# The borders between layers 0, 1 and 2: the last eight k-tiles by token halves, the norm per token block, and the first 768 columns turned in parts

## What is computed

```python
for layer in range(DEPTH):                    # 0: dilated attention, 1: latent attention
    y = mixer(x, ...)                         # h = x @ w_in ... y @ w_out
    x = layer_norm(DEEPNORM_ALPHA * x + y, ln_g[layer], ln_b[layer])
for layer in range(DEPTH):                    # layers 2 and 3 of the kernel
    x = x + layer(x, ev_norm or od_norm, ...) # RMS norm ahead of w_in
```

## Time and profile before

| | |
|---|---|
| median of 3 runs | 2440.97 us (2440.07 to 2441.13) |
| the profiled execution | 2441.87 us, span 2440.1 us, mean granted TensorE clock 0.999 |
| TensorE matmul busy | 2419.8 us, 99% of the span, 12720 |
| TensorE weight load busy | 2064.6 us, 85% |
| VectorE busy | 1474.5 us, 60%; of it 953.0 in L1853 |
| ScalarE busy | 1184.4 us, 49%; of it 802.0 in L1261 |
| GpSimd busy | 144.6 us, 6%; of it 97.0 in L2687 |
| DMA | 416.68 MB, mean 171 GB/s |

### The profile page before, as it was taken

One profiled execution on the slowest core, in us unless ns is written; L12 is line 12 of the kernel. 1 busy time (PEld: TensorE's weight loads), 2 busy tenths in 40 slices (PEclk: granted clock), 3 DMA queues, 4 the chain that ended last, 5 costly groups with the idle time before them and its releaser, 6 DMA issues.

```text
span 2440.1 us, 31500 instructions
## 1 busy us (share of the span) xinstructions
PE 2419.8 (99%) x12720; PEld 2064.6 (85%) x12720; DVE 1474.5 (60%) x1936; ACT 1184.4 (49%) x1620; POOL 144.6 (6%) x124
## 2 busy tenths in 40 slices
PE   8999999999999999999999999999999999999999
PEld 7888888888888888888899878888888888888887
DVE  5747575757575757575556575555455566657654
ACT  5454444444444445344555455554444468645443
POOL 1101010101010101000000000000000010000000
PEclk9999999999999999999999999999999999999999
DMA  8555555555554555646554656555555564433344
GB/s 261 173 173 195 197 187 164 190 165 187 166 189 159 187 172 173 207 147 199 172 138 134 203 153 194 173 184 184 176 173 161 169 209 155 138 111 125 111 138 138
DMA packets 368469, 416.68 MB, mean 171 GB/s; under 512 B 28042, under 2 KB 298596, under 8 KB 367812
## 3 DMA queue, kind: packets, MB, share of 16 engines
q1 hardware_dynamic: 366692, 407.72, 52.4%
q0 software_dynamic: 1344, 6.89, 0.8%
q10 hardware_dynamic: 288, 0.05, 0.0%
HBM read 412.52 MB, written 2.10 MB: 170 GB/s over the span
## 4 chain that ended last, share of the span: by engine, by line
PE 96%; ACT 2%; DVE 1%; issue 1%; DMA 0%; POOL 0%; ACTq 0%; DVEq 0%
PE ps L617 19%; PE ps L619 19%; PE ps L618 19%; PE ps L648 15%; PE ps L647 7%; PE ps L1129 2%; PE ps L689 2%; PE ps L851 1%; PE ps L840 1%; PE ps L902 1%; PE ps L904 1%; PE ps L903 1%; PE ps L845 1%; PE ps L719 1%; PE ps L939 0%
## 5 line engine op out<-in xcount | busy, mean ns | idle before, releaser
L1853 DVE TENSOR_TENSOR wlo<-raw,whi 128x1024 fp32r<-128x1024 f32 (+1 forms) x768 | 953.0, 1250 | 637.6 <-ACT whi L1261 634.4
L1261 ACT CAST whi<-raw 128x1024 fp32r<-128x1024 f32 (+1 forms) x774 | 802.0, 1041 | 730.6 <-PE ps L619 545.2
L617 PE MATMUL ps<-whi,xx 128*128 128x512 f32 x2088 | 833.9, 399 | 0.0
L619 PE MATMUL ps<-whi,xx 128*128 128x512 f32 x2088 | 815.5, 391 | 0.0
L618 PE MATMUL ps<-wlo,xx 128*128 128x512 f32 x2088 | 814.3, 390 | 0.0
L648 PE MATMUL ps<-xx,whi 128*128 128x512 f32 x1536 | 538.9, 396 | 0.0
L619 PEld LDWEIGHTS ps<-whi,xx 128*128 128x128 f32 x2088 | 392.4, 188 | 83.6
L617 PEld LDWEIGHTS ps<-whi,xx 128*128 128x128 f32 x2088 | 393.1, 188 | 78.1 <-issue 1.6
L618 PEld LDWEIGHTS ps<-wlo,xx 128*128 128x128 f32 x2088 | 393.2, 188 | 76.4
L647 PE MATMUL ps<-xx,wlo 128*128 128x256 f32 x1440 | 405.7, 282 | 0.0
L648 PEld LDWEIGHTS ps<-xx,whi 128*128 128x128 f32 x1536 | 286.2, 188 | 63.2
(11 more groups left out here) (407 smaller groups left out, 1862.2 us busy)
## 6 DMA issues: line engine op xcount, KB each, us to landing
raw<-in_dsa_w_in SPq DMA_DIRECT2D x320, 512.0 KB, 4.5
raw<-in_ev_w_in SPq DMA_DIRECT2D x144, 512.0 KB, 4.6
raw<-in_od_w_in SPq DMA_DIRECT2D x96, 512.0 KB, 4.5
raw<-in_mla_w_in SPq DMA_DIRECT2D x48, 512.0 KB, 4.3
raw<-in_dsa_w_out SPq DMA_DIRECT2D x32, 512.0 KB, 4.6
raw<-in_mla_w_out SPq DMA_DIRECT2D x32, 512.0 KB, 4.8
raw<-in_ev_w_out SPq DMA_DIRECT2D x32, 512.0 KB, 4.6
raw<-in_od_w_out SPq DMA_DIRECT2D x32, 512.0 KB, 4.9
```

The source lines that it names most:

```text
L617: pe.matmul(o, xh[:, k, tokens[tb]], hi, start=start and s + l == 0, stop=False)
L619: m = pe.matmul(o, xl[:, k, tokens[tb]], hi, start=False, stop=stop and s + l == 2)
L1261: act.copy(whi[:, h % 4, :, 0:n] if n > FEW else few_high(h, n), whole_half(raw[:, u % 4, 2 * (h % 2):2 * (h % 2) + 2], n)).then_inc(hi_do ...
L1853: dve.tensor_tensor(wlo[:, h % 4, :, 0:n] if n > FEW else few_low(h, n), whole_half(raw[:, h // 2 % 4, 2 * (h % 2):2 * (h % 2) + 2], n), h ...
```

## The change

It touches the two borders 0 to 1 and 1 to 2.

- `last_unit` becomes `last_units` there: the last eight k-tiles of the last slab (four weight halves) run first for token block 0, then for block 1. Inside the second pass stand the transposes of parts (0, 0) and (1, 0) of the next layer's input. A part (g, tb) is pair g for token block tb; there are parts for g = 0, 1, 2 (`PARTS` = 3, 768 columns).
- Add, statistics, variance, power and shift are done for each block on its own (`measured`, `shift`).
- All columns are normed on ScalarE. The 768 first columns are turned without factor and bias; these are then applied behind the transposes, where they are numbers per partition: by ScalarE into `xh`, by VectorE into a scratch copy in `y` (`exact`), from which `xh` is subtracted. The numbers come from `vec`, for which four more rows are loaded early in layer 0; for layer 2 VectorE multiplies them once by the RMS gain.
- The same factor and bias on `x` itself, for the residual, move to GpSimd for the 768 columns: two instructions on 2 x 768 columns behind the transposes of part (2, 1). `add(0)` and `add(1)` of the layer, and `squares(2)`, wait for them.
- TensorE's slab takes pairs 0 to 2 for block 0, then for block 1, then 3 to 7 as before. `keep_warm` is not called there.

The diff, cut to its core:

```diff
+        def exact(g, tb):
+            o = (PARTS * tb + g) * S
+            return y[:, 0, o:o + S].rearrange("p (l t) -> p l t", l=2)
+
+        def part_of_bank(g, tb, l):
+            o = tb * S + l * P
+            return ps[:, 4 + g, o:o + P]
...
+            def turn_part(layer, g, tb):
+                pe.wait_ge(*ln_a.at(layer - 1, f"n{g}{tb}"))
+                for l in range(2):
+                    k = 2 * g + l
+                    m = pe.transpose(part_of_bank(g, tb, l), x[:, tb, k * P:(k + 1) * P], ident[:, :])
+                m.then_inc(*xt_p.up("t"))
+
             def first_slab(layer):
-                keep_warm(14, 7)
-                turn_x(layer, (0,))
-                keep_warm(6, 7)
-                for g in range(8):
+                def three(h, g, l, tb):
+                    k = 2 * g + l
+                    o, hi, lo = ps[:, tb, :], whi[:, h % 4, l], wlo[:, h % 4, l]
+                    pe.matmul(o, xh[:, k, tokens[tb]], hi, start=k == 0, stop=False)
+                    pe.matmul(o, xh[:, k, tokens[tb]], lo, start=False, stop=False)
+                    return pe.matmul(o, xl[:, k, tokens[tb]], hi, start=False, stop=k == KT - 1)
+
+                for g in range(PARTS):
+                    h = half[0] + g
+                    pe.wait_ge(*xt_d.at(xt_turn(layer, g, 0), "lo"))
+                    pe.wait_ge(lo_done, h + 1)
+                    three(h, g, 0, 0)
+                    if g == 2:
+                        turn_part(layer, 0, 1)
+                    three(h, g, 1, 0)
+                    if g == 0:
+                        turn_part(layer, 2, 0)
+                turn_part(layer, 1, 1)
+                for g in range(PARTS):
+                    pe.wait_ge(*xt_d.at(xt_turn(layer, g, 1), "lo"))
+                    three(half[0], g, 0, 1)
+                    three(half[0], g, 1, 1).then_inc(half_done, 1)
+                    half[0] += 1
+                    if g == 0:
+                        turn_part(layer, 2, 1)
+                    else:
+                        turn_x(layer, (g + 2,))
+                for g in range(PARTS, 8):
                     h = half[0]
-                    pe.wait_ge(*xt_d.at(8 * layer + g, "lo"))
+                    pe.wait_ge(*xt_d.at(xt_turn(layer, g), "lo"))
                     pe.wait_ge(lo_done, h + 1)
                     for l in range(2):
-                        k = 2 * g + l
-                        hi, lo = whi[:, h % 4, l], wlo[:, h % 4, l]
                         for tb in range(TB):
-                            o = ps[:, tb, :]
-                            pe.matmul(o, xh[:, k, tokens[tb]], hi, start=k == 0, stop=False)
-                            pe.matmul(o, xh[:, k, tokens[tb]], lo, start=False, stop=False)
-                            m = pe.matmul(o, xl[:, k, tokens[tb]], hi, start=False, stop=k == KT - 1)
-                        if k == 0:
-                            turn_x(layer, (1,))
+                            m = three(h, g, l, tb)
                     m.then_inc(half_done, 1)
                     half[0] += 1
                     if g < 6:
...
+            def last_units(k0, bank, layer):
+
+                for tb in range(TB):
+                    for s in range(4):
+                        h = half[0] + s
+                        pe.wait_ge(lo_done, h + 1)
+                        for l in range(2):
+                            k = k0 + 2 * s + l
+                            hi, lo = whi[:, h % 4, l], wlo[:, h % 4, l]
+                            o = ps[:, bank + tb, :]
+                            pe.matmul(o, xh[:, k, tokens[tb]], hi, start=False, stop=False)
+                            pe.matmul(o, xh[:, k, tokens[tb]], lo, start=False, stop=False)
+                            m = pe.matmul(o, xl[:, k, tokens[tb]], hi, start=False, stop=k == KT - 1)
+                            if tb and l == 0 and s >= 2:
+                                turn_part(layer + 1, s - 2, 0)
+                        if tb:
+                            m.then_inc(half_done, 1)
+                    if tb == 0:
+                        m.then_inc(*out_p.up("half"))
+                half[0] += 4
+
...
                     if layer == 2 or s == 0:
                         project(nothing, N, out_bank(s), fine=fine, then=turning_x(3) if s else None)
                         continue
-                    for j in range(3):
+                    for j in range(3 if layer == 3 else 2):
                         unit(nothing, 4 * j, N, out_bank(s), j == 0, False, fine)
-                    last_unit(12, out_bank(s))
+                    if layer == 3:
+                        last_unit(12, out_bank(s))
+                    else:
+                        last_units(8, out_bank(s), layer)
...
                 for u in range(8):
                     unit(side, fine, {0: more, 4: late}.get(u))
                 for s in range(2):
-                    project(nothing, fine, turning_x(3) if layer == 2 and s else None)
+                    if layer >= 2 or s == 0:
+                        project(nothing, fine, turning_x(3) if layer == 2 and s else None)
+                        continue
+                    for j in range(2):
+                        unit(nothing, fine)
+                    split(half[0] + AHEAD)
+                    half[0] += 4
             def first_slab(layer):
-                def normalise(q, tb):
-                    v = x[:, tb, q * N:(q + 1) * N]
+                def normalised(tb, c):
+                    v = x[:, tb, c]
                     return act.activation(v, v, ACT.Identity, bias=hrstd[:, tb:tb + 1], scale=rstd[:, tb:tb + 1])
-
-                act.wait_ge(*st_d.at(layer - 1, "h"))
-                normalise(1, 0)
-                turn_x(layer, (0,))
-                normalise(1, 1).then_inc(*ln_a.up("q0"))
-                normalise(2, 0)
-                normalise(2, 1).then_inc(*ln_a.up("q1"))
-                normalise(3, 0)
-                turn_x(layer, (1,))
-                normalise(3, 1).then_inc(*ln_a.up("q2"))
+                def part(g, tb):
+                    normalised(tb, slice(g * S, (g + 1) * S)).then_inc(*ln_a.up(f"n{g}{tb}"))
+
+                def quarter(q):
+                    for tb in range(TB):
+                        m = normalised(tb, slice(max(q * N, PARTS * S), (q + 1) * N))
+                    m.then_inc(*ln_a.up(f"q{q - 1}"))
+
+                def turned(g, tb):
+                    act.wait_ge(*xt_p.at(xt_turn(layer, g, tb), "t"))
+                    for l in range(2):
+                        k = 2 * g + l
+                        m = act.activation(xh[:, k, tokens[tb]], part_of_bank(g, tb, l), ACT.Identity,
+                                           bias=part_bias(layer, k), scale=part_gain(layer, k))
+                    m.then_inc(*xt_a.up("hi"))
+
+                split(half[0])
+                act.wait_ge(*st_d.at(layer - 1, "h0"))
+                act.wait_ge(*setup_d.at(0, "bias"))
+                part(0, 0)
+                split(half[0] + 1)
+                part(1, 0)
+                turned(0, 0)
+                turned(1, 0)
+                part(2, 0)
+                split(half[0] + 2)
+                turned(2, 0)
+                act.wait_ge(*st_d.at(layer - 1, "h1"))
+                part(0, 1)
+                part(1, 1)
+                turned(0, 1)
+                part(2, 1)
+                turned(1, 1)
+                quarter(1)
                 for g in range(8):
                     split(half[0] + AHEAD)
                     half[0] += 1
-                    if g < 6:
+                    if g == 0:
+                        turned(2, 1)
+                    elif g < 6:
                         turn_x(layer, (g + 2,))
+                    if g < 2:
+                        quarter(g + 2)
...
+                    elif layer < 3 and q < 2:
+                        dve.wait_ge(*ln_g.at(layer - 1, "bias"))
...
+                def measured(tb):
+                    c = slice(3 * N, D)
+                    if tb == 0:
+                        dve.wait_ge(*out_p.at(turn, "half"))
+                    else:
+                        dve.wait_ge(half_done, half[0])
+                    if turn == 0:
+                        dve.wait_ge(rows_in[3], 16)
+                    dve.scalar_tensor_tensor(out=x[:, tb, c], in0=x[:, tb, c], scalar=ALPHA, in1=ps[:, out_bank(3) + tb, :],
+                                             op0=ALU.mult, op1=ALU.add).then_inc(*add_d.up(f"add{3 + tb}"))
+                    dve.wait_ge(*add_d.at(turn, f"add{3 + tb}"))
+                    dve.bn_stats(stats[:, tb, 3], x[:, tb, c]).then_inc(*st_d.up(f"stats{tb}"))
+                    dve.wait_ge(*st_d.at(turn, f"stats{tb}"))
+                    dve.bn_aggr(mv[:, tb, :], flat(stats[:, tb])).then_inc(*st_d.up(f"aggr{tb}"))
+                    dve.wait_ge(*st_d.at(turn, f"aggr{tb}"))
```

(64 more changed lines are left out.)

82 lines of the change are left out of this document (40 added, 42 removed).

## The result

The changed kernel takes 2454.79 us (median of 5 runs, 2453.75 to 2455.46), the kernel before 2440.21 beside it: a ratio of 1.0058 [1.0047, 1.0068], 14.6 us slower. The profiled execution has a span of 2452.4 us and a mean granted clock of 0.996.

The account below looks back on a forecast made before the run. TensorE was taken to bound the kernel (96% of the last chain), with hardly any VectorE slack behind its filler. Terms 5.75 + 5.0 + 2 x 1.2 = 13.15 us, against the median 2440.97, gave 2454; range 2446 to 2460.

Parts of the forecast that it names:

- GpSimd's two instructions: Behind transposes (2,1), factor and bias of 1536 elements per partition each run 3.4 us, bounds 3.1 and 3.9.
- TensorE's idle: TensorE stands idle before the six matmuls of (2,1), some 7.2 us at each boundary.
- Pair g=3: Start of slab pair g=3, 5.75 us later than before at the first boundary, 5.0 at the second.
- the walk: Instruction-by-instruction costing of the new order from the last product to slab pair g=3, at each boundary.
- hold: GpSimd's two instructions block VectorE's SBUF work for their whole length, 3.4 us each, at each boundary.
- The walk without GpSimd: New order alone, up to pair g=3: gains 0.5 us at the first boundary, 1.2 at the second.
- Clock: Half clock behind TensorE's idle costs 1.2 us per boundary, between nothing and 2.0 with 0.1 behind it.
- The sum: Both boundaries' delays plus clock: 5.75 + 5.0 + 2 x 1.2 = 13.15 us, giving 2454.
- What costs nothing: Four more small loads and two tiny VectorE products early in layer 0 cost nothing, covered by over 20 us.
- (a): Rival: no mutual exclusion of GpSimd and VectorE bites at the boundaries; -1.7 us, 2439.3, chance 0.08.
- (b): Rival: filler time simply gone, TensorE goes from product to slab without a wait; -12 us, 2429, chance 0.03.
- (c): Rival: GpSimd gives the ports up between pieces of about 512 elements, or half overlaps PSUM work; +4.2, 2445, chance 0.08.

Follow-up runs that it names:

- e9: Changed kernel with GpSimd's two instructions released by the low part of pair 7, in layer 2 behind the relative-bias load's issue; 2447.44 us, ratio 1.0029.
- e8: Kernel before, plus two GpSimd multiplications of 1536 elements on scratch data, released by the bias of pair 3 in each slab; 2452.36 us, ratio 1.005.
- e3: Changed kernel with 26 identity matmuls of 128x128 ahead of TensorE's wait for the low part (2,1); 2452.22 us, ratio 1.0049.
- e1: Changed kernel with GpSimd's factor and bias applied to one column per token block instead of 768; 2441.49 us, ratio 1.0006.
- e5: Kernel of e2 with layer 2's relative-bias load issued behind x7 again instead of behind x2; 2441.42 us, ratio 1.0005.
- e6: Kernel of e5 with shift(1) right behind turned(1,0) and transposes (0,1) and (1,1) moved from pair 2 to pair 1; 2436.76 us, ratio 0.9986.
- e4: Changed kernel with each of GpSimd's two instructions cut into three of 512 elements; 2453.75 us.
- e2: Changed kernel with factor and bias of the first 768 columns moved from GpSimd to VectorE, behind pair 7's; 2449.46 us, ratio 1.0038.

## Why the prediction was right, step by step

The forecast was 2454.0 and the time 2454.79. The mechanism and its place were right; that the sum came out closer than its terms is luck.

- **GpSimd's two instructions.** Forecast: 3.4 us each, bounds 3.1 to 3.9, behind the end of the VectorE instruction that they wait for. Measured so, the factor takes 3.32 behind L2123 (1075.23 to 1078.55) and the bias 3.29 behind the split (1079.63 to 1082.92); with the waiting they show as 3.62 and 4.28. e9's factor at the second border begins as VectorE falls idle and takes 3.50. So the scaling of the row with 512 elements held for three times the size. e8's multiplication, with one region as both sources and target, is shorter, 2.75.
- **VectorE.** Forecast: a split and the subtraction of turned(2,1) stretched, the PSUM operations between them not. Exactly that: 4.48, 0.72, 2.89.
- **TensorE's idle.** Forecast 7.2 at each border, measured 6.69 and 6.67.
- **Pair g=3.** Forecast +5.75 and +5.0, without the clock; measured +6.7 and +5.9, of which e3 puts 0.3 and 0.2 down to the clock. The rest of the gap is the walk, below, 1.2 too short at each border, against a hold of 5.8 (e3 less e1) where the forecast had 6.2.
- **The walk without GpSimd.** Forecast -0.5 and -1.2; e1 gave +0.7 and -0.05. This is the step that was off, by 2.3 us together. `turned` was put at 0.94 on VectorE: start to start it takes 1.10 (0.76 and 0.34), six times, so 6.6 us and not the 5.6 of the forecast. ScalarE's pair for it was put at 0.63: its rows show 0.81. Against that, the power of one column takes 0.57, not the 0.90 of two, so that transposes (0,0) come 0.24 late where I had 0.6. The waits in block 0 came out at 0.60, 1.04 and 0.56 for 0.55, 1.2 and 0.5, the one for (0,1) at 1.31 for 0.9. On the walk's own scale e1 starts (0,1) at 1072.4 for 1071.4 and g=3 at 1080.1 for 1079.0, so nearly all of the error is made ahead of block 1. Behind it the walk has a wait of about 0.95 before (2,1), as in e1 (0.96), and one of some 1.4 before g=3 (0.97).
- **Clock.** Forecast 1.2 per border, bounds 0 to 2.1. By e3's medians 2.6 in all, by its timelines 0.3 and 1.1. So the size lies between half of the forecast and all of it. In the first border the recovery (full at about 1086.6, 3.3 us behind the restart) was much quicker than the 7.4 us of the earlier trace rows, and the slow matmuls fell where VectorE was late anyway.
- **The sum.** By the ruler 13.5 (forecast 13.15): about 0.6 for the order, 11.5 for the hold, 1.4 for the clock. The forecast had -1.7, 12.45 and 2.4. Two errors of some 2 us, of opposite sign, and they need not have met. By the medians the difference is 14.6, missed by 1.4; that 2454.0 lies only 0.8 from 2454.79 owes something to the kernel before, which came out at 2440.21 beside it and not at 2440.97.
- **What costs nothing.** The small loads and products early in layer 0 left no trace: in e1 TensorE's waits outside the borders are those of before.
- **Rivals.** (a) No exclusion: refuted by e1 and e8. Its 2439.3 is the time without the hold, for which e1 gives 2441.5. (b) Filler time simply gone, 2429: e1 and e5 show that without the hold the gain is nil, because the filler time comes back as waits on a busy VectorE. e6 ends 3.2 us below the kernel before by moving one 0.15 us instruction and two pairs of transposes. (c) The hold given up in pieces: refuted by the stretched instructions of after; e4, with pieces in fact, shows that even then nearly nothing is gained. It also took shorter idle times as free of clock, and e4's 2.38 us at the first border was not.

The exact sizes of three things stay open: the clock's share (1.4 or 2.6), the shares of e6's two moves, and how much of e9's 6 us over e1 is its TensorE wait (3.96) and how much the half clock behind it (0.53, 0.50, 0.50 and 0.76 over the windows from 1466 to 1474, an estimate of 3 us at most).

## What to carry to other kernels

Work moved to GpSimd didn't run beside VectorE where both read SBUF: each such instruction took its length out of VectorE's queue, less what VectorE's PSUM operations filled. So look whether VectorE has slack just there, and put the work where it has (in the later pairs of the slab, six operations on VectorE itself cost nothing). Filler time between two stages is a sign that a chain of other engines is as long as it; before counting it as a gain, walk that chain and look for the short instruction that is queued last but waited for first. And when a step is moved, list what stands behind every wait that moves with it, the DMA issues too: twice here (e2, e9) the loss began there.

## What the hardware showed that I had not expected

- A GpSimd memset of 1536 elements (1.38 us) leaves VectorE's two-source instructions alone; a copy of the same size, about as long (1.47 us), holds them as a multiplication does.
- The hold also reaches VectorE's one-source copies from SBUF to SBUF. In e9 the two copies of the relative bias took 3.08 us beside GpSimd's bias, 1.83 without it:

```profile
1459.72 3.08 DVE L2513 COPY work<-work 128x1024 f32<-128x1024 f32 x2 [2.41 <-DMA work<-in_ev_rel_bias]
```

- TensorE's clock came back at different speeds after similar idle times: 3.3 us behind the restart at the first border of after, some 5.6 at the second. At one and the same place in layer 3, half clock lasted some 6.8 us in before and in e1, and 3.4 in after. An idle time of 2.38 us lowered the clock at the first border of e4 and not at the second; waits of up to 1.31 in e1, one behind another, did not lower it.
- The load of the relative bias through GpSimd's queue landed some 9 us after its issue began (1455.85 to 1464.97 in e2).
